# One exponential over both maps' score banks in pass B of the prompt attention

## The chip, the cores and the metric

The kernel runs on one core of a Trainium2 chip. The core has four compute engines that matter here, each with an instruction queue of its own that is worked off in order: TensorE (PE in the profile; its weight loads are PEld), VectorE (DVE), ScalarE (ACT) and GpSimd (POOL). SyncE (SP) issues most DMAs. Engines wait for each other by semaphores. The metric is the device time of one execution in microseconds. Over three runs the kernel before took 2607.59 us (median; 2605.26 to 2613.81).

## The reference, cut to what matters

One step of a hybrid encoder layer: a normalization, one large input projection, two kinds of attention (FoX heads with a cumulative forget bias; differential heads with two softmax maps, a relative bias and a chunk mask), gates, two projections up, one out, a normalization. It is computed for a prompt of 2048 tokens and for 8 sampled sequences of 16 tokens. The change is in the prompt's attention, whose core is, for 8 FoX heads of 64 channels and for 4 differential heads with two maps:

```
s = q . k * SCALE + (c_query - c_key)          # FoX, causal
p = softmax(s); o = p @ v

s_m = q_m . k_m * SCALE + bias(k - q)          # differential, m = 0, 1, masked by chunks of 64
a = softmax(s_0) - lam * softmax(s_1); o = a @ v
```

All arithmetic is in float32; matmul inputs are split into high and low parts where one pass isn't exact enough.

## The kernel before, in words

Three parts follow each other with some overlap: `project` (input projection, the sampled sequences), `prompt_attention`, and `merge` (gates and output). `prompt_attention` works through 8 pairs f. An even f is a pair of FoX heads, an odd f is the two maps of one differential head; in both cases a pair has two maps m = 0, 1. Each pair has 4 blocks of 512 queries (QUERIES), so 32 blocks b.

Pass A takes 128 queries by up to 1024 keys at a time (`A_UNITS`), with queries on partitions, to find each query's maximum (and for differential heads the sum of exponentials): score matmuls in `scores_a` (lines 2064 to 2069) into two PSUM tensors `sa`, band addition (line 1952) and maximum (line 1955) on VectorE, exponential with a sum on ScalarE (line 1891, differential heads only). The result becomes a row added to the queries' data, so that pass B's scores come out already shifted.

Pass B has keys on partitions. A unit u is one block of 512 queries by one tile of 128 keys (`B_UNITS`; 320 of them, 4, 8, 12 and 16 in the four blocks of a pair). For both maps:

1. `scores_b` (lines 2086, 2087): two matmuls a map into `sb_[m]`, a PSUM bank of 512 float32 columns each; near the diagonal only 384 or 256 columns.
2. For differential units near the diagonal (`in_band`, 76 units), VectorE adds a bias band of 256 or 128 columns to each map's scores in place (line 2001).
3. ScalarE writes the exponential of each bank to SBUF, `e[:, u % 6, m]` (line 1924).
4. FoX: GpSimd masks the diagonal square (line 1843), VectorE sums over key tiles (lines 2024, 2027), and `product` multiplies both maps by their values (line 2111). Differential: VectorE combines both maps into `w` (line 2008), and one product follows (line 2108).

There is one pair of banks `sb_`, so unit u + 1 can write bank m only after the exponential of unit u has read it. `e_made` counts exponentials, two a unit, and `scores_b` waits for `2 * u + m - 1`, map by map.

The order on every engine is written out in `events()` (lines 1601 to 1698) as one list that all engines walk through: scores ("B", u) and exponential ("E", u), "W" of unit u - 1, the sums "R" of unit u - 2, as many pass A units ("A", with its exponential "X" one unit later) as a rate asks for, then products. A differential unit's product comes two units later, a FoX unit's in pairs behind every second unit (lines 1686 to 1690).

Of the kernel before, what the change touches and what calls it, by code (L numbers as in the profile page):

```python
# [1481 lines left out]
def prompt_attention(nc, d, keep, link):  # L1482
# [12 lines left out]
    with ExitStack() as space:  # L1495
        s.ctx = space
        with ExitStack() as small:
            s.ctx = small
            with ExitStack() as early:
                lam_prod = Scope(nc, early, "a_", keep).sb("lam_prod", [P, 2, HD])  # L1500
            nmax, total = s.sb("nmax", [P, 2, 2, 8]), s.sb("total", [P, 2, 2, 8])
            nm, gap, log_sum, const = (s.sb(n, [P, 2, 8]) for n in ("nm", "gap", "log_sum", "const"))
            scaled_sum = s.sb("scaled_sum", [P, 2, 8])
            c_hi, c_lo = s.sb("c_hi", [8, P], F32R), s.sb("c_lo", [8, P], F32R)
            ident, ident16 = s.sb("ident", [P, P]), s.sb("ident16", [P, P], BF16)
            lam_in, lam = s.sb("lam_in", [P, 4, HD]), s.sb("lam", [P, 8])
            causal = s.sb("causal", [P, 1, P], BF16)
            v = [s.sb("v0", [P, PROMPT_TILES, P])]
            link["v0"] = v[0]
            run = s.sb("run", [P, 2, MAPS, QUERIES])  # L1510
            ones = s.sb("ones", [P, HD])
            o_raw, o_inv = s.sb("o_raw", [P, QUERIES]), s.sb("o_inv", [P, QUERIES])
        s.ctx = space
        s.sb("space", [P, 6 * D_MODEL])
        maps.append([[s.sb(f"{n}_1{m}", [P, SEQ], F32R) for m in range(MAPS)] for n in ("q1", "k1", "q2", "k2")])
        q1, k1, q2, k2 = ([maps[f][n] for f in range(2)] for n in range(4))
        e = s.sb("e", [P, E_SLOTS, MAPS, QUERIES])
        w = s.sb("w", [P, W_SLOTS, QUERIES])
        o = s.sb("o", [P, 2, QUERIES])
        v.append(s.sb("v1", [P, PROMPT_TILES, P]))  # L1520
        band = s.sb("band", [P, 2, BAND])
        s.sb("space_b", [P, BAND])
        sa = [s.ps(f"sa{i}", [P, CHUNK_KEYS]) for i in range(2)]
        cT = s.ps("cT", [P, 512])
        op = s.ps("op", [P, QUERIES])
        sb_ = [s.ps(f"sb{m}", [P, QUERIES]) for m in range(MAPS)]
    yield

    maps_in = [[s.sem(f"maps_in{f}{m}") for m in range(MAPS)] for f in range(2)]
# [202 lines left out]
    def sync(sp, events):  # L1732
        def load_side(f):

            z = f % 2
            if f % 2:
                for layout in range(2):
                    sp.dma_start(band[:, layout, :], d["band"][layout, f // 2]).then_inc(side_in[z], 16)
            else:
                if f == 0:  # L1740
                    sp.wait_ge(ones_set[0], 4)
                for m in range(MAPS):
                    sp.dma_start(k2[z][m][HD:HD + 2, :].bitcast(F32), d["nck"][f + m]).then_inc(side_in[z], 16)

        def load_map(f, m, n):

            z, hi, lo = f % 2, slice(0, HD), slice(HD, P)
            rows = slice(m * HD, (m + 1) * HD)
            tensor, part, x = ((q1, hi, "q_hi"), (k1, hi, "k_lo"), (q1, lo, "q_lo"), (k1, lo, "k_hi"),
                               (q2, hi, "q_hi"), (k2, hi, "k_hi"))[n]  # L1750
            sp.dma_start(tensor[z][m][part, :].bitcast(F32), d[x][pair_of(f), rows, :]).then_inc(maps_in[z][m], 16)

        def load_v(f):

            z = f % 2
            vsrc, col = d["diff_v_p"] if f % 2 else d["fox_v_p"], f // 2
            if f >= 2:
                sp.wait_ge(multiplied, (f - 1) * NUF)
            sp.dma_start(v[z][:], vsrc.rearrange("(t p) n -> p t n", p=P)
                         [:, :, col * P:(col + 1) * P]).then_inc(v_in[z], 16)  # L1760

        def load(f):

            load_side(f)
            for m in range(MAPS):
                for n in range(6):
                    load_map(f, m, n)
            load_v(f)

        for ev in events:  # L1770
            if ev == ("I", 0):
                sp.dma_start(ident[:], d["ident"]).then_inc(const_in, 16)
                for n, name in enumerate(("lambda_q1", "lambda_k1", "lambda_q2", "lambda_k2")):
                    sp.dma_start(lam_in[:, n, :], d[name].to_broadcast([P, HD])).then_inc(const_in, 16)
            elif ev[0] == "MERGE":
                link["merge"]["sync"](sp, [ev[1]])
            elif ev[0] == "LS":
                load_side(ev[1])
            elif ev[0] == "LM":
                load_map(*ev[1:])  # L1780
            elif ev[0] == "LV":
                load_v(ev[1])
            elif ev == ("I", 1):
                load(1)
            elif ev[0] == "L" and ev[2] == 0:
                f = ev[1]
                sp.wait_ge(b_scored, (f - 1) * 2 * NUF)
                load(f)
            elif ev[0] == "O":
                b = ev[1]  # L1790
                f, Q = b // BLOCKS, b % BLOCKS
                if is_diff(b):
                    sp.wait_ge(o_made, b + 1 - n_total[b + 1])
                else:
                    sp.wait_ge(o_divided, n_total[b + 1])
                sp.dma_start(d["oT"][pair_of(f), :, Q * QUERIES:(Q + 1) * QUERIES], o[:, b % 2, :]).then_inc(stored[b % 2], 16)

    def gpsimd(pool, events):
        for ev in events:
# [33 lines left out]
                pool.wait_ge(o_divided, n_total[b + 1])  # L1833
            elif ev[0] == "E" and on_edge(*B_UNITS[ev[1]]):
                u = ev[1]
                pool.wait_ge(e_made, 2 * u + 2)
                if n_edge[u]:
                    pool.wait_ge(e_masked, n_edge[u])
                else:
# [15 lines left out]
    def scalar(act, events):  # L1855
        for ev in events:
# [52 lines left out]
            elif ev[0] == "E":  # L1909
                u = ev[1]  # L1910
                cols = valid(u)
                for m in range(MAPS):
                    if in_band(*B_UNITS[u]):
                        act.wait_ge(b_biased, 2 * n_band[u] + m + 1)
                    else:
                        act.wait_ge(b_scored, 2 * u + m + 1)
                    if m == 0 and u >= E_SLOTS:

                        if is_diff(B_UNITS[u - E_SLOTS][0]):
                            act.wait_ge(w_made, n_diff[u - E_SLOTS + 1])  # L1920
                        else:
                            act.wait_ge(multiplied, u - E_SLOTS + 1)
                            act.wait_ge(e_added, n_added[u - E_SLOTS + (2 if B_UNITS[u - E_SLOTS][1] == 0 else 1)])
                    nc.scalar.activation(e[:, u % E_SLOTS, m, cols], sb_[m][:, cols], ACT.Exp).then_inc(e_made, 1)  # L1924

    def vector(dve, events):
        for ev in events:
# [65 lines left out]
            elif ev[0] == "E" and in_band(*B_UNITS[ev[1]]):  # L1993
# [2 lines left out]
                lo, hi = max(t0, 0) * P, min(t0 + 2, 4) * P  # L1996
                if t0 <= 0:
                    dve.wait_ge(side_in[1], side_total(B_UNITS[u][0] // BLOCKS))
                for m in range(MAPS):
                    dve.wait_ge(b_scored, 2 * u + m + 1)  # L2000
                    nc.vector.tensor_tensor(sb_[m][:, lo:hi], sb_[m][:, lo:hi], band[:, 1, lo - t0 * P:hi - t0 * P],
                                            ALU.add).then_inc(b_biased, 1)
            elif ev[0] == "W" and is_diff(B_UNITS[ev[1]][0]):
                u = ev[1]
                cols = valid(u)
                dve.wait_ge(e_made, 2 * u + 2)
                dve.wait_ge(multiplied, u - W_SLOTS + 1)
                nc.vector.scalar_tensor_tensor(w[:, u % W_SLOTS, cols], e[:, u % E_SLOTS, 1, cols], lam[:, 5:6],
                                               e[:, u % E_SLOTS, 0, cols], ALU.mult, ALU.add).then_inc(w_made, 1)
            elif ev[0] == "R" and not is_diff(B_UNITS[ev[1]][0]) and B_UNITS[ev[1]][1] > 0:  # L2010
# [1 line left out]
                b, kt = B_UNITS[u]  # L2012
                cols, n = valid(u), n_total[b] % 2
                now, sum_ = e[:, u % E_SLOTS, :, cols], run[:, n, :, cols]
                dve.wait_ge(e_made, 2 * u + 2)
                if on_edge(b, kt):
                    dve.wait_ge(e_masked, n_edge[u + 1])
                if kt == 1:
# [17 lines left out]
    def tensor(pe, events):  # L2036
# [35 lines left out]
        def scores_b(u):  # L2072
# [5 lines left out]
            r = max(0, kt - 4 * Q)  # L2078
            c0 = min(r, 2) * P
            ks = slice(kt * P, (kt + 1) * P)  # L2080
            for m in range(MAPS):
                if u:
                    pe.wait_ge(e_made, 2 * u + m - 1)
                out = sb_[m][:, c0:QUERIES]
                qs = slice(Q * QUERIES + c0, (Q + 1) * QUERIES)
                nc.tensor.matmul(out, k1[z][m][:, ks], q1[z][m][:, qs], start=True, stop=False)  # L2086
                nc.tensor.matmul(out, k2[z][m][0:ROW_C + 2, ks], q2[z][m][0:ROW_C + 2, qs], start=False,  # L2087
                                 stop=True).then_inc(b_scored, 1)

        def product(u):  # L2090
            b, kt = B_UNITS[u]
            z, Q = b // BLOCKS % 2, b % BLOCKS
            if is_diff(b):
                pe.wait_ge(w_made, n_diff[u + 1])
            else:
                pe.wait_ge(e_made, 2 * u + 2)
                if on_edge(b, kt):
                    pe.wait_ge(e_masked, n_edge[u + 1])
            if kt == 0 and b % BLOCKS == 0:
# [48 lines left out]

    def pair_done(sp):

        sp.wait_ge(b_scored, (FT - 1) * 2 * NUF)
        sp.wait_ge(multiplied, (FT - 1) * NUF)

    def first_stored(sp):
# [126 lines left out]
```

## Time and profile before

| | |
|---|---|
| median of 3 runs | 2607.59 us |
| the profiled execution: its own time | 2605.0 us |
| its span, first to last instruction | 2603.2 us |
| mean granted TensorE clock | 0.984 |
| busy: PE, DVE, ACT, POOL | 2478.4, 1374.3, 942.9, 386.0 us |
| line 1924 (pass B's exponentials) | 640 instructions, 310.4 us |
| line 2001 (pass B's band additions) | 152 instructions |
| lines 2086 and 2087 (pass B's scores) | 640 each, 276.5 and 237.1 us |

The profile is of one execution. Times of instructions are from the hardware's records; the ends of matmuls are modelled, since they are pipelined, and the busy time of an engine counts what overlaps once. Pass B runs from 1312 to 2196 us of the span. A clock of 1.00 is 2.4 GHz; the granted clock has two levels, 2.4 and 1.2 GHz, and a number between is the mean over a stretch.

### The profile page before, as it was taken

The page shows a single profiled execution, that of the slowest core. Times are in us where ns is not written, and L with a number is a line of the kernel's source. Part 1 is how long each engine was busy: PE and PEld are TensorE (multiplying, and loading weights), DVE is VectorE, ACT ScalarE, POOL GpSimd, SP SyncE. Part 2 cuts the span into 40 slices and gives each one's busy share as a digit, 9 for nine tenths or more (in the row PEclk, how much of TensorE's full clock was granted, in tenths as well). Part 3 has the DMA queues.
Part 4 walks back from the last instruction along what each step waited for, and adds up shares of the span by engine and source line. Part 5 has one row for each costly group of instructions (what it writes and reads, how often), then busy time and mean ns, then how long its engine had stood idle before and what let it go on. Part 6 is the DMA issues. An engine that isn't in the chain of part 4 may idle for free.

```text
span 2603.2 us, 35097 instructions
## 1 busy us (share of the span) xinstructions
PE 2478.4 (95%) x13569; PEld 1977.2 (76%) x13569; DVE 1374.3 (53%) x2227; ACT 942.9 (36%) x1869; POOL 386.0 (15%) x398
## 2 busy tenths in 40 slices
PE   7999999999999999999988899899899989999998
PEld 5788888789999999999855565565565556888897
DVE  5311123315443333542368888788788786655553
ACT  4123331112222222111136645654664666322221
POOL 0100001121100000112352113103212242000000
PEclk9999999999999999999989999999999999999999
DMA  5688888958987666888560523235054023544432
GB/s 153 161 223 207 202 210 206 209 138 243 244 237 226 207 215 181 233 206 175 145 158 9 126 50 89 55 77 130 5 131 107 28 83 108 181 133 130 143 118 89
DMA packets 583892, 388.65 MB, mean 149 GB/s; under 512 B 318672, under 2 KB 538776, under 8 KB 577416
## 3 DMA queue, kind: packets, MB, share of 16 engines
q1 hardware_dynamic: 574592, 367.80, 53.8%
q0 software_dynamic: 9136, 18.63, 2.1%
q8 instruction: 107, 1.75, 0.3%
q14 instruction: 57, 0.47, 0.1%
HBM read 284.83 MB, written 134.79 MB: 161 GB/s over the span
## 4 chain that ended last, share of the span: by engine, by line
PE 75%; DVE 6%; SPq 5%; ACT 5%; issue 4%; DMA 3%; POOL 1%; DVEq 0%; ACTq 0%; POOLq 0%
PE p_acc L876 13%; PE p_acc L881 12%; PE p_acc L880 12%; PE a_op L2111 5%; PE a_sb L2086 4%; PE a_sb L2087 3%; PE a_op L2108 3%; PE a_sa L2064 2%; PE a_sa L2067 2%; PE e_U L1428 2%; PE e_U L1430 2%; PE e_U L1429 2%; ACT a_e L1924 2%; DVE a_nmax L1955 2%; PE a_sa L2065 2%
## 5 line engine op out<-in xcount | busy, mean ns | idle before, releaser
L876 PE MATMUL p_acc<-p_h_hi,p_w_hi 128*128 128x384 f32 (+1 forms) x1960 | 716.1, 365 | 11.9 <-DVE p_ev L586 5.5
L881 PE MATMUL p_acc<-p_h_hi,p_w_lo 128*128 128x384 f32 (+1 forms) x1920 | 688.0, 358 | 0.0
L880 PE MATMUL p_acc<-p_h_lo,p_w_hi 128*128 128x384 f32 (+1 forms) x1920 | 687.8, 358 | 0.0
L1955 DVE TENSOR_REDUCE a_nmax<-a_sa 128x1 f32<-128x1024 f32 (+7 forms) x384 | 347.2, 911 | 125.0 <-PE a_sa L2069 45.1
L1924 ACT ACTIVATE a_e<-a_sb 128x512 f32<-128x512 f32 (+3 forms) x640 | 310.4, 533 | 278.5 <-PE a_sb L2087 183.8
L876 PEld LDWEIGHTS p_acc<-p_h_hi,p_w_hi 128*128 128x128 f32 x1960 | 370.8, 189 | 52.7 <-issue 12.8
L881 PEld LDWEIGHTS p_acc<-p_h_hi,p_w_lo 128*128 128x128 f32 x1920 | 362.1, 189 | 30.4
L880 PEld LDWEIGHTS p_acc<-p_h_lo,p_w_hi 128*128 128x128 f32 x1920 | 362.6, 189 | 29.0
L692 DVE TENSOR_TENSOR p_w_lo<-p_raw,p_w_hi 128x1024 fp32r<-128x1024 f32 x96 | 125.6, 1308 | 368.8 <-ACT p_w_hi L619 368.7
L2086 PE MATMUL a_sb<-a_q,a_k 128*128 128x512 f32 (+2 forms) x640 | 276.5, 436 | 20.6 <-ACT a_e L1924 18.1
L2087 PE MATMUL a_sb<-a_q,a_k 68*128 68x512 f32 (+2 forms) x640 | 237.1, 374 | 0.0
L619 ACT CAST p_w_hi<-p_raw 128x1024 fp32r<-128x1024 f32 x98 | 102.4, 1045 | 337.8 <-DMA p_raw<-in_w_in 253.4
L599 POOL TENSOR_SCALAR p_ev_hi<-p_ev 128x896 fp32r<-128x896 f32 (+1 forms) x32 | 35.6, 1113 | 1164.3 <-DVE p_ev L586 910.5
L2086 PEld LDWEIGHTS a_sb<-a_q,a_k 128*128 128x128 f32 x640 | 124.0, 194 | 107.6 <-ACT a_e L1924 52.4
L1891 ACT ACTIVATE a_sa<-a_sa,a_nmax 128x1024 f32<-128x1024 f32 (+4 forms) x192 | 162.3, 846 | 51.8 <-DVE a_nmax L1955 50.7
L2064 PE MATMUL a_sa<-a_k,a_q 128*128 128x512 f32 (+4 forms) x320 | 131.5, 413 | 41.3 <-ACT a_sa L1891 41.2
L2111 PE MATMUL a_op<-a_e,a_v 128*64 128x512 f32 (+3 forms) x640 | 145.9, 570 | 3.6 <-issue 3.6
L2108 PE MATMUL a_op<-a_w,a_v 128*128 128x512 f32 (+3 forms) x320 | 147.1, 541 | 1.3 <-ACT a_o_raw L1883 0.8
L2087 PEld LDWEIGHTS a_sb<-a_q,a_k 68*128 68x128 f32 x640 | 124.2, 194 | 23.1 <-issue 10.1
L574 ACT ACTIVATE p_ev<-p_acc 128x384 f32<-128x384 f32 (+1 forms) x80 | 42.8, 534 | 271.9 <-PE p_acc L881 271.8
L2064 PEld LDWEIGHTS a_sa<-a_k,a_q 128*128 128x128 f32 x320 | 61.7, 193 | 100.4 <-ACT a_sa L1891 76.9
L2027 DVE TENSOR_TENSOR a_run<-a_run,a_e 128x1024 f32<-128x1024 f32 (+3 forms) x128 | 137.2, 1072 | 0.6
(233 smaller groups left out, 3475.6 us busy)
## 6 DMA issues: line engine op xcount, KB each, us to landing
p_raw<-in_w_in SPq DMA_DIRECT2D x98, 512.0 KB, 5.7
s_k_raw<-scratch_kS SPq DMA_DIRECT2D x64, 512.0 KB, 6.9
scratch_kS<-in_cache_fox_k SPq DMA_DIRECT2D x32, 512.0 KB, 6.6
scratch_kS<-in_cache_diff_k SPq DMA_DIRECT2D x32, 512.0 KB, 6.4
s_v_raw<-in_cache_fox_v SPq DMA_DIRECT2D x8, 2048.0 KB, 11.0
s_v_raw<-in_cache_diff_v SPq DMA_DIRECT2D x8, 2048.0 KB, 10.0
a_q<-scratch_q_hi SPq DMA_DIRECT2D x32, 512.0 KB, 13.3
a_k<-scratch_k_hi SPq DMA_DIRECT2D x32, 512.0 KB, 15.2
```

Source lines behind the costliest of these rows:

```text
L876: nc.tensor.matmul(acc[a % 2][:, 0:n], hi, h_hi[p][:, k, at:at + n], start=(k == 0), stop=False)
L880: nc.tensor.matmul(acc[a % 2][:, 0:n], hi, h_lo[p][:, k, at:at + n], start=False, stop=False)
L881: last = nc.tensor.matmul(acc[a % 2][:, 0:n], lo, h_hi[p][:, k, at:at + n], start=False, stop=(k == DK - 1))
L1891: nc.scalar.activation(scores_of(ev[1]), scores_of(ev[1]), ACT.Exp, bias=nmax[:, b % 2, c, col:col + 1], accum_out=total[:, b % 2, c, col: ...
L1924: nc.scalar.activation(e[:, u % E_SLOTS, m, cols], sb_[m][:, cols], ACT.Exp).then_inc(e_made, 1)
L1955: nc.vector.tensor_reduce(nmax[:, b % 2, c, col:col + 1], scores_of(ev[1]), axes, ALU.max, negate=True).then_inc(a_maxed, 1)
L2027: nc.vector.tensor_tensor(sum_, sum_, now, ALU.add).then_inc(e_added, 1)
L2064: nc.tensor.matmul(out, q1[z][m][:, qs], k1[z][m][:, k0:k0 + wide], start=True, stop=False)
L2086: nc.tensor.matmul(out, k1[z][m][:, ks], q1[z][m][:, qs], start=True, stop=False)
L2087: nc.tensor.matmul(out, k2[z][m][0:ROW_C + 2, ks], q2[z][m][0:ROW_C + 2, qs], start=False, stop=True).then_inc(b_scored, 1)
L2108: last = nc.tensor.matmul(op[:, cols], v[z][:, kt, :], w[:, u % W_SLOTS, cols], start=(kt == 0), stop=final)
L2111: last = nc.tensor.matmul(op[m * HD:(m + 1) * HD, cols], v[z][:, kt, m * HD:(m + 1) * HD], e[:, u % E_SLOTS, m, cols], start=(kt == 0), st ...
```

## The change

The two score banks become one tensor `sb` of 2 x 512 columns over two adjacent banks. One exponential instruction reads both maps and writes both; one band addition covers both maps, its band operand repeated for the second. The score matmuls are the same four, but one semaphore count, after the last, stands for the unit, and one wait, for the whole exponential of the unit before, stands ahead of the first. Counts of `b_scored`, `e_made` and `b_biased` are halved where they are waited for.

```diff
-        sb_ = [s.ps(f"sb{m}", [P, QUERIES]) for m in range(MAPS)]
+        sb_ = s.ps("sb", [P, MAPS, QUERIES])
...
-                for m in range(MAPS):
-                    if in_band(*B_UNITS[u]):
-                        act.wait_ge(b_biased, 2 * n_band[u] + m + 1)
+                if in_band(*B_UNITS[u]):
+                    act.wait_ge(b_biased, n_band[u + 1])
+                else:
+                    act.wait_ge(b_scored, u + 1)
...
-                    nc.scalar.activation(e[:, u % E_SLOTS, m, cols], sb_[m][:, cols], ACT.Exp).then_inc(e_made, 1)
+                nc.scalar.activation(e[:, u % E_SLOTS, :, cols], sb_[:, :, cols], ACT.Exp).then_inc(e_made, 1)
...
-                for m in range(MAPS):
-                    dve.wait_ge(b_scored, 2 * u + m + 1)
-                    nc.vector.tensor_tensor(sb_[m][:, lo:hi], sb_[m][:, lo:hi], band[:, 1, lo - t0 * P:hi - t0 * P],
-                                            ALU.add).then_inc(b_biased, 1)
+                dve.wait_ge(b_scored, u + 1)
+                bias = band[:, 1:2, lo - t0 * P:hi - t0 * P].to_broadcast([P, MAPS, hi - lo])
+                nc.vector.tensor_tensor(sb_[:, :, lo:hi], sb_[:, :, lo:hi], bias, ALU.add).then_inc(b_biased, 1)
...
+            if u:
+                pe.wait_ge(e_made, u)
             for m in range(MAPS):
-                if u:
-                    pe.wait_ge(e_made, 2 * u + m - 1)
-                out = sb_[m][:, c0:QUERIES]
+                out = sb_[:, m, c0:QUERIES]
...
-                nc.tensor.matmul(out, k2[z][m][0:ROW_C + 2, ks], q2[z][m][0:ROW_C + 2, qs], start=False,
-                                 stop=True).then_inc(b_scored, 1)
+                last = nc.tensor.matmul(out, k2[z][m][0:ROW_C + 2, ks], q2[z][m][0:ROW_C + 2, qs], start=False,
+                                 stop=True)
+            last.then_inc(b_scored, 1)
```

The other edits put `u + 1` for `2 * u + 2` and `NUF` for `2 * NUF` in the waits of GpSimd's mask, VectorE's `w` and sums, the products and SyncE's loads.

## Rows read from the trace of the kernel before

**Rows 1.** The page, part 1: busy time, share of the span, instructions.
```profile
span 2603.2 us, 35097 instructions
PE 2478.4 (95%) x13569; PEld 1977.2 (76%) x13569; DVE 1374.3 (53%) x2227; ACT 942.9 (36%) x1869; POOL 386.0 (15%) x398
```

**Rows 2.** Busy time by stretch, pass B; us busy (instructions) per engine, clock, DMA.
```profile
1312.00:2196.00 884.00, 808.24 (x3374) 488.49 (x3374) 716.37 (x1132) 520.77 (x1134) 227.15 (x275) 0.97 0.34 81
```

**Rows 3.** Waits of TensorE in that stretch: us in total, times, longest.
```profile
PE a_sa L2064 <- ACT a_sa L1891: 41.2, 49, 1.9
PE a_sb L2086 <- ACT a_e L1924: 18.1, 29, 1.2
...
PE a_op L2111 <- issue: 3.6, 1, 3.6
...
PE a_sb L2086 <- DMA a_q<-a_c_lo: 2.3, 1, 2.3
```

**Rows 4.** Groups by line and shape, same stretch: count | busy us, mean ns.
```profile
L1924 ACT ACTIVATE a_e<-a_sb 128x512 f32<-128x512 f32 x448 | 243.7, 597 | 190.0 <-PE a_sb L2087 141.9 <-DVE a_sb L2001 47.4
...
L1891 ACT ACTIVATE a_sa<-a_sa,a_nmax 128x1024 f32<-128x1024 f32 x80 | 87.8, 1097 | 9.1 <-DVE a_nmax L1955 8.8
...
L2001 DVE TENSOR_TENSOR a_sb<-a_sb,a_band 128x256 f32<-128x256 f32 x96 | 37.5, 425 | 5.0 <-PE a_sb L2087 4.5
...
L1924 ACT ACTIVATE a_e<-a_sb 128x384 f32<-128x384 f32 x64 | 28.6, 491 | 25.1 <-PE a_sb L2087 13.8 <-DVE a_sb L2001 10.6
...
L2001 DVE TENSOR_TENSOR a_sb<-a_sb,a_band 128x128 f32<-128x128 f32 x56 | 15.0, 293 | 4.0 <-PE a_sb L2087 2.3
...
L1891 ACT ACTIVATE a_sa<-a_sa,a_nmax 128x512 f32<-128x512 f32 x16 | 10.6, 664 | 6.3 <-DVE a_nmax L1955 6.3
```

**Rows 5.** Timeline, two FoX gaps: start us, us, engine, line.
```profile
1423.25 0.40 PE L2087 MATMUL a_sb<-a_q,a_k 68*128 68x512 f32 x1
...
1424.65 0.40 PE L2087 MATMUL a_sb<-a_q,a_k 68*128 68x512 f32 x1
...
1425.09 1.08 ACT L1924 ACTIVATE a_e<-a_sb 128x512 f32<-128x512 f32 x2 [0.33 <-PE a_sb L2087]
1425.12 0.40 PE L2087 MATMUL a_sb<-a_q,a_k 68*128 68x512 f32 x1
...
1425.80 1.94 PE L2111 MATMUL a_op<-a_e,a_v 128*64 128x512 f32 x8
```

**Rows 6.** Timeline, a differential gap with products alone.
```profile
1490.21 0.39 PE L2087 MATMUL a_sb<-a_q,a_k 68*128 68x512 f32 x1
...
1490.44 1.02 PE L2108 MATMUL a_op<-a_w,a_v 128*128 128x512 f32 x2
...
1491.53 0.39 PE L2087 MATMUL a_sb<-a_q,a_k 68*128 68x512 f32 x1
```

**Rows 7.** Timeline, a gap of a banded differential unit.
```profile
1499.08 0.40 PE L2087 MATMUL a_sb<-a_q,a_k 68*128 68x512 f32 x1
...
1499.12 0.83 DVE L2001 TENSOR_TENSOR a_sb<-a_sb,a_band 128x256 f32<-128x256 f32 x2
...
1501.06 0.34 PE L2087 MATMUL a_sb<-a_q,a_k 68*128 68x384 f32 x1
```

**Rows 8.** Timeline, TensorE released by an exponential (first row: ScalarE's alone).
```profile
1362.11 0.62 ACT L1924 ACTIVATE a_e<-a_sb 128x512 f32<-128x512 f32 x1
...
1362.78 0.50 PE L2086 MATMUL a_sb<-a_q,a_k 128*128 128x512 f32 x1 [0.78 <-ACT a_e L1924]
...
1363.12 0.40 PE L2087 MATMUL a_sb<-a_q,a_k 68*128 68x512 f32 x1
```

**Rows 9.** Busy time by stretch, as rows 2: pass B's start, and behind it.
```profile
1312.00:1441.00 129.00, 112.48 (x484) 64.11 (x484) 100.61 (x131) 69.97 (x156) 51.73 (x52) 0.93 0.32 75
...
2210.00:2590.00 380.00, 376.10 (x1935) 337.57 (x1936) 203.29 (x415) 106.79 (x259) 19.70 (x35) 1.00 0.43 136
```

More of the change, by code:

```diff
@@ L1786, in sync @@
                 f = ev[1]
-                sp.wait_ge(b_scored, (f - 1) * 2 * NUF)
+                sp.wait_ge(b_scored, (f - 1) * NUF)
                 load(f)
@@ L1835, in gpsimd @@
                 u = ev[1]
-                pool.wait_ge(e_made, 2 * u + 2)
+                pool.wait_ge(e_made, u + 1)
                 if n_edge[u]:
@@ L1911, in scalar @@
                 cols = valid(u)
-                for m in range(MAPS):
-                    if in_band(*B_UNITS[u]):
-                        act.wait_ge(b_biased, 2 * n_band[u] + m + 1)
-                    else:
[L1916 to L1923, printed above, removed]
-                    nc.scalar.activation(e[:, u % E_SLOTS, m, cols], sb_[m][:, cols], ACT.Exp).then_inc(e_made, 1)
+                if in_band(*B_UNITS[u]):
+                    act.wait_ge(b_biased, n_band[u + 1])
+                else:
+                    act.wait_ge(b_scored, u + 1)
+                if u >= E_SLOTS:
+                    if is_diff(B_UNITS[u - E_SLOTS][0]):
+                        act.wait_ge(w_made, n_diff[u - E_SLOTS + 1])
+                    else:
+                        act.wait_ge(multiplied, u - E_SLOTS + 1)
+                        act.wait_ge(e_added, n_added[u - E_SLOTS + (2 if B_UNITS[u - E_SLOTS][1] == 0 else 1)])
+                nc.scalar.activation(e[:, u % E_SLOTS, :, cols], sb_[:, :, cols], ACT.Exp).then_inc(e_made, 1)
     def vector(dve, events):
@@ L2005, in vector @@
                 cols = valid(u)
-                dve.wait_ge(e_made, 2 * u + 2)
+                dve.wait_ge(e_made, u + 1)
                 dve.wait_ge(multiplied, u - W_SLOTS + 1)
@@ L2014, in vector @@
                 now, sum_ = e[:, u % E_SLOTS, :, cols], run[:, n, :, cols]
-                dve.wait_ge(e_made, 2 * u + 2)
+                dve.wait_ge(e_made, u + 1)
                 if on_edge(b, kt):
@@ L2095, in product @@
             else:
-                pe.wait_ge(e_made, 2 * u + 2)
+                pe.wait_ge(e_made, u + 1)
                 if on_edge(b, kt):
@@ L2149, in pair_done @@
     def pair_done(sp):
-        sp.wait_ge(b_scored, (FT - 1) * 2 * NUF)
+        sp.wait_ge(b_scored, (FT - 1) * NUF)
         sp.wait_ge(multiplied, (FT - 1) * NUF)
```

## The prediction

> **What bounds the kernel now.** I read the page first. TensorE is busy for 95% of the span, ScalarE for 36% [rows 1], so what a change does to the time is what it does to TensorE's queue. The changed instructions (lines 1924, 2001, 2086, 2087) all lie between 1312 and 2196 us, the stretch in which pass B runs its 320 units. The busy times of that stretch alone come next: TensorE 808.2 of 884 us, VectorE 716.4, ScalarE 520.8 [rows 2]. TensorE therefore stands idle there for 884.0 - 808.2 = 75.8 us, and has 2.76 us a unit; VectorE follows closely, ScalarE has room. Third, the waits of TensorE in the stretch: 41.2 us for pass A's exponentials (line 1891), only 18.1 us for pass B's own exponentials (line 1924) [rows 3]. Today the two score banks work as a pair. While ScalarE exponentiates bank 0, TensorE fills bank 1, and it may fill bank 0 for the next unit while bank 1 is exponentiated. So a unit's exponentials are nearly over when TensorE is through with its scores: the pair of them starts at 1425.09, 0.03 us before the last score matmul starts, and ends 0.65 us after that matmul's end [rows 5].
>
> **The change, part by part.**
>
> *The exponential.* 640 instructions become 320. One of 512 columns takes 597 ns, one of 384 takes 491 [rows 4]: 106 ns for 128 columns. A fused one of 2 x 512 is then 597 + 4 x 106 = 1021 ns; from pass A's two sizes (1097 less 664 = 433 ns for 512 columns, [rows 4]) it is 1030. I take 1.03 us. The ends are 1.02 and the 1.10 of pass A's own instruction. The pair takes 1.08 today [rows 5], so ScalarE is relieved by 0.05 us a unit, 16 us in all, of an engine that is busy for 59% of the stretch: worth nothing on the path by itself.
>
> *The waits.* This is where the cost is. The exponential of a unit can't start before all four score matmuls, and the next unit's scores can't start before it is over. Behind the waiting score matmul, in TensorE's queue, stand the other map's scores, pass A's next scores and the value products; behind pass A's scores VectorE's maxima wait. What TensorE can still do meanwhile is what the written order puts between two score blocks: pass A's scores and products. To price one gap I measure from the end of a unit's last score matmul to the end of the next unit's first line-2087 matmul (ends, because the recorded start of a matmul in a full stream lies early). The change needs for it: 0.04 us until ScalarE starts (first-map scores end 1425.05, the pair starts 1425.09, [rows 5]); 1.03 for the exponential; 0.05 until TensorE restarts (an exponential ends at 1362.11 + 0.62 = 1362.73, the released matmul starts at 1362.78); 0.74 for the two matmuls (1362.78 to 1363.12 + 0.40) [rows 8]. That is 1.86 us for a full-width unit. What each kind of gap has today:
>
> FoX unit without a product behind it [rows 5]: 1423.25 + 0.40 = 1423.65 to 1424.65 + 0.40 = 1425.05, so 1.40 us, 0.46 too little. The next gap of the same rows holds the eight product matmuls of two units (1.94 us) and covers everything; so it is with every second FoX unit. Differential unit with products alone [rows 6]: 1490.60 to 1491.92, 1.32 us, 0.54 too little. With pass A's scores as well the gap is mostly between 1.6 and 2.1, where the price is small or nothing.
>
> *The band addition.* In a banded unit it stands between scores and exponential. 425 ns for 256 columns, 293 for 128 [rows 4], so 132 ns for 128 more, and 0.69 us for 2 x 256. Two take 0.83 today [rows 7]. VectorE saves 0.14 us in most of the 76 banded units, some 10 us of its 716. But the first addition now starts after the second map's scores. In rows 7 the gap runs from 1499.48 to 1501.40, 1.92 us; needed are 0.04 + 0.69 + 0.06 between the engines (estimated from the lag of ScalarE behind TensorE, above) + 1.03 + 0.05 + 0.63 (narrower matmuls) = 2.50: 0.58 too little. Where VectorE is late anyway with its maxima, less is lost.
>
> *The sum.* I went through the timeline gap by gap for all 319, with the needs above cut to each unit's width, and with ScalarE's and VectorE's earlier work where it ends later than the scores:
> FoX, 160 gaps: 62 are too short, on average 1.26 us where 1.75 is needed: 30.8 us.
> Differential without band, 84 gaps: 45 too short, 1.62 against 1.95: 14.8 us.
> Differential with band, 75 gaps: 51 too short, 1.94 against 2.41: 23.9 us.
> Together 69.5 us in 158 gaps; the other 161 cost nothing. It takes the place of nothing: the present waits on line 1924 are inside the measured gaps.
>
> *What hangs on it.* (a) A unit's last exponential ends 0.04 + 1.03 = 1.07 us behind the scores and not 0.65, so pass A's exponential, next in ScalarE's queue, starts 0.42 us later. TensorE waits for that one 49 times, for 41.2 us [rows 3]. Bounds: nothing where VectorE's maximum is the later one, 49 x 0.42 = 21 us if never; I take 6. (b) Idle time of TensorE that a delay eats up, because its releaser does not move: GpSimd's mask before the first product (3.6 us), DMA (2.3), [rows 3]. Bounds 0 and, if pass A's waits gave way too, 47 us; I take 5, since those waits stand behind the very exponentials that move. (c) The clock. The granted clock is 0.93 of full speed in the stretch with 13% of TensorE's time idle, 1.00 where it is 1% [rows 9]: part of such a stretch runs at 1.2 instead of 2.4 GHz. Bounds: nothing, and 23 us if the time at the lower level doubles with the idle time (0.03 of 884 us lost today). I take 5.
> DMA, SP's and GpSimd's instructions stay; their waits are renumbered and come at the same point of the work, or 0.4 us later for the mask, which is used two units on.
>
> Sum: 69.5 + 6 - 5 + 5 = 75.5 us. The profiled execution took 2605.0 us (span 2603.2): 2680.5. The median of the runs lies 2.6 above it, so the forecast is 2683 us.
>
> The row for ScalarE shows 59% of the stretch. On this the Trainium skill, "Perfetto Trace Analysis", section "Optimizing Scalar/DVE Operations", says two things: grouping into larger operations helps throughput if the engine is saturated, and if it isn't but makes bubbles on other engines, breaking instructions up may let work finish sooner. By the first alone the sum would be the 16 us of relief; by the second it is the loss above. The trace bears out the second: the released engine is the full one.
>
> **The rivals.**
> *A: the cover holds (not slower).* ScalarE and VectorE set the pace: TensorE's 75.8 us of idle time and VectorE's 81% speak for it. Then the shorter queues are what counts: 49 waits x 0.05 = 2 us, and 10 us of band additions: 2593 to 2608. It decides where a gap is longer than its need; against it stand 158 gaps that aren't.
> *B: half eaten up.* Later units find their other waits gone: the 57.7 us of TensorE's idle time that isn't for line 1924 falls by half, 29 us in place of (b)'s 5: 2683 - 24 = 2659. Against it: delay ahead of pass A's scores delays their exponentials too.
> *C: the delay multiplies.* ScalarE's queue carries it: (a) at 21 us, and each FoX gap with pass A's work becomes ScalarE-bound: about 15 + 15 more, 2713.
> *D: the clock.* With idle time twice today's, TensorE stays at 1.2 GHz twice as long: (c) at 23, 2701. For it, the 0.93 of rows 9.
> The Trainium skill, "TensorE: Matmul & The Clock Gate", section "A second HAM failure mode: psum-queue depth-cycling", tells of the same case: short idle spells between groups of matmuls that cycle through PSUM make the clock swing between its two levels. Rows 9 show both levels, but not yet that spells under a microsecond bring the lower one.
>
> **How the numbers follow.** Forecast 0.60, A 0.04, B 0.14, C 0.10, D 0.12. The likeliest gives 2683. Low end: B's absorption and nothing for (a) and (c): 2607.6 + 69.5 - 29 - 5 = 2643. High end: C with two thirds of D's 18 us: 2725. Some 2 in 10 are left outside, A among them. A measurement of this kernel tells some 0.3% (8 us) from no change. Only A reaches that near: slower 0.95, same 0.03, faster 0.02.
>
> **What would show it.** The wait of line 2086 on line 1924 grows from 18 us to 80 or more, in single waits of 0.3 to 0.9 us, in FoX units every second one; the fused exponential lasts 1.02 to 1.04 us at full width; TensorE's idle time in the stretch rises to 145 to 155 us with the same matmul work; the stretches before 1312 us and after pass B keep their length. The forecast is wrong if the wait of line 2086 stays under 40 us, if pass A's wait (41.2 us) falls by more than it says, or if the clock in the stretch falls under 0.94.

## The result, and the profile after

The changed kernel takes 2694.64 us (median of 4 runs, 2687.03 to 2702.71) against 2609.54 for the kernel before in the same comparison: ratio 1.0327, 95% interval 1.0306 to 1.0348, so 85 us slower. The forecast was 2683.

The page, part 1, answers to [rows 1]:

```profile
span 2688.7 us, 34701 instructions
PE 2515.7 (94%) x13569; PEld 1985.1 (74%) x13569; DVE 1374.5 (51%) x2151; ACT 920.2 (34%) x1549; POOL 380.8 (14%) x398
```

The matmuls are as many as before, ScalarE has 320 instructions fewer, VectorE 76, and the span is 85.5 us longer. Pass B now runs from 1312 to 2282 us. Busy time by stretch (columns as in [rows 2]) and TensorE's waits in it (as [rows 3]):

```profile
1312.00:2282.00 970.00, 846.03 (x3375) 497.96 (x3374) 714.83 (x1057) 497.52 (x813) 221.77 (x275) 0.94 0.31 74
```

```profile
PE a_sb L2084 <- ACT a_e L1923: 66.6, 118, 1.4
PE a_sa L2062 <- ACT a_sa L1891: 42.6, 33, 2.6
...
PE a_sa L2065 <- DVE a_nmax L1954: 3.7, 4, 1.1
```

The stretch is 86 us longer than in [rows 2], all of the loss. TensorE's wait for pass B's exponentials grows from 18.1 us in 29 waits to 66.6 in 118. But TensorE's idle time grows only by 48 us (75.8 to 124.0). The other 38 us are recorded as busy time: the same matmuls take longer. Part of that is the clock, 0.94 where it was 0.97; summed over its steps TensorE spends 109 us of the stretch at 1.2 GHz and spent 61. Half of that increase lies in the first pair of heads (41 us against 17), where the clock was 0.93 in [rows 9]:

```profile
1312.00:1458.00 146.00, 124.18 (x481) 69.66 (x480) 100.99 (x131) 66.08 (x115) 49.63 (x52) 0.86 0.28 66
```

The groups by line and shape, as [rows 4]:

```profile
L1923 ACT ACTIVATE a_e<-a_sb 128x1024 f32<-128x1024 f32 x224 | 229.5, 1024 | 287.6 <-PE a_sb L2085 222.3 <-DVE a_sb L2000 60.9 <-DVE a_w L2006 3.9
...
L2000 DVE TENSOR_TENSOR a_sb<-a_sb,a_band 128x512 f32<-128x512 f32 x48 | 33.4, 696 | 22.3 <-PE a_sb L2085 21.8
```

The full-width exponential takes 1024 ns and the full-width addition 696, where 1030 and 689 had been worked out.

The first gap of [rows 5] in the timeline after (block 3, key tile 10, counted from 0; rows left out are marked):

```profile
1439.07 0.40 PE L2085 MATMUL a_sb<-a_q,a_k 68*128 68x512 f32 x1
...
1439.50 1.02 ACT L1923 ACTIVATE a_e<-a_sb 128x1024 f32<-128x1024 f32 x1 [1.11 <-PE a_sb L2085]
...
1439.77 0.40 PE L2062 MATMUL a_sa<-a_k,a_q 128*128 128x512 f32 x1
...
1440.00 0.39 PE L2063 MATMUL a_sa<-a_k,a_q 66*128 66x512 f32 x1
1440.42 0.44 ACT L1891 ACTIVATE a_sa<-a_sa,a_nmax 128x256 f32<-128x256 f32 x1
...
1440.58 0.50 PE L2084 MATMUL a_sb<-a_q,a_k 128*128 128x512 f32 x1 [0.19 <-ACT a_e L1923]
...
1440.91 0.40 PE L2085 MATMUL a_sb<-a_q,a_k 68*128 68x512 f32 x1
```

From the last score's end (1439.07 + 0.40) to the end of the next unit's first map (1440.91 + 0.40) it is 1.84 us, where it was 1.40 and 1.86 was said to be needed. TensorE has its pass A scores in that time and then nothing, and 0.19 us is all that the row names as waiting. The rest is hidden in how matmuls are recorded. In a full stream they start 0.23 us apart though each is recorded as 0.40 long (1439.77 and 1440.00), so the record before a pause covers some 0.17 us of it; and the released matmul is recorded as 0.50 us and not 0.40. So a loss of 0.44 us shows as 0.19 us of wait. The same in the gap of [rows 6]:

```profile
1509.76 0.40 PE L2085 MATMUL a_sb<-a_q,a_k 68*128 68x512 f32 x1
...
1510.20 1.02 ACT L1923 ACTIVATE a_e<-a_sb 128x1024 f32<-128x1024 f32 x1 [1.20 <-PE a_sb L2085]
...
1511.27 0.50 PE L2084 MATMUL a_sb<-a_q,a_k 128*128 128x512 f32 x1 [0.25 <-ACT a_e L1923]
1511.62 0.40 PE L2085 MATMUL a_sb<-a_q,a_k 68*128 68x512 f32 x1
```

1510.16 to 1512.02 is 1.86 us (1.32 before). And the banded gap of [rows 7]:

```profile
1519.68 0.40 PE L2085 MATMUL a_sb<-a_q,a_k 68*128 68x512 f32 x1
...
1520.19 0.70 DVE L2000 TENSOR_TENSOR a_sb<-a_sb,a_band 128x512 f32<-128x512 f32 x1 [0.85 <-PE a_sb L2085]
...
1520.92 1.02 ACT L1923 ACTIVATE a_e<-a_sb 128x1024 f32<-128x1024 f32 x1 [2.11 <-DVE a_sb L2000]
...
1522.28 0.34 PE L2085 MATMUL a_sb<-a_q,a_k 68*128 68x384 f32 x1
```

1520.08 to 1522.62 is 2.54 us (1.92 before; 2.50 said).

### The profile page after: what moved, and what is told of

Read it like the earlier page. It is cut to its first block, busy times and chain, and to the rows that moved or that the text cites. A ratio compares the mean times of both kernels' runs of the same rounds, so it can differ in the third digit from the quotient of the medians.

```text
span 2688.7 us, 34701 instructions
## 1 busy us (share of the span) xinstructions
PE 2515.7 (94%) x13569; PEld 1985.1 (74%) x13569; DVE 1374.5 (51%) x2151; ACT 920.2 (34%) x1549; POOL 380.8 (14%) x398
## 4 chain that ended last, share of the span: by engine, by line
PE 71%; ACT 7%; SPq 7%; DVE 6%; issue 4%; DMA 3%; POOL 1%; DVEq 0%; ACTq 0%; POOLq 0%
PE p_acc L876 11%; PE p_acc L881 11%; PE p_acc L880 11%; PE a_sb L2084 5%; PE a_op L2110 5%; ACT a_e L1923 5%; PE a_sb L2085 4%; SPq L355 3%; PE a_sa L2062 2%; PE e_U L1428 2%; PE e_U L1430 2%; PE e_U L1429 2%; PE a_op L2107 2%; PE a_sa L2065 2%; DVE a_nmax L1954 2%
## 5 line engine op out<-in xcount | busy, mean ns | idle before, releaser
L1923 ACT ACTIVATE a_e<-a_sb 128x1024 f32<-128x1024 f32 (+1 forms) x320 | 286.7, 896 | 402.6 <-PE a_sb L2085 278.5
L881 PEld LDWEIGHTS p_acc<-p_h_hi,p_w_lo 128*128 128x128 f32 x1920 | 362.0, 189 | 30.7
L2084 PE MATMUL a_sb<-a_q,a_k 128*128 128x512 f32 (+2 forms) x640 | 270.0, 426 | 67.6 <-ACT a_e L1923 66.6
L2062 PE MATMUL a_sa<-a_k,a_q 128*128 128x512 f32 (+4 forms) x320 | 133.3, 418 | 44.1 <-ACT a_sa L1891 42.6
L2110 PE MATMUL a_op<-a_e,a_v 128*64 128x512 f32 (+3 forms) x640 | 156.2, 605 | 2.7 <-issue 2.7
L2085 PEld LDWEIGHTS a_sb<-a_q,a_k 68*128 68x128 f32 x640 | 126.0, 197 | 16.1 <-issue 2.7
```

Of the source, the lines that this page charges most:

```text
L881: last = nc.tensor.matmul(acc[a % 2][:, 0:n], lo, h_hi[p][:, k, at:at + n], start=False, stop=(k == DK - 1))
L1923: nc.scalar.activation(e[:, u % E_SLOTS, :, cols], sb_[:, :, cols], ACT.Exp).then_inc(e_made, 1)
L2062: nc.tensor.matmul(out, q1[z][m][:, qs], k1[z][m][:, k0:k0 + wide], start=True, stop=False)
L2085: last = nc.tensor.matmul(out, k2[z][m][0:ROW_C + 2, ks], q2[z][m][0:ROW_C + 2, qs], start=False, stop=True)
L2110: last = nc.tensor.matmul(op[m * HD:(m + 1) * HD, cols], v[z][:, kt, m * HD:(m + 1) * HD], e[:, u % E_SLOTS, m, cols], start=(kt == 0), st ...
```

## The experiments

Two theories were tried throughout. G: a gap costs what the chain "scores, exponential, scores" needs beyond the work that TensorE has there. Q: the later exponential pushes back pass A's exponentials in ScalarE's queue, and these hold TensorE. The expectations name further ones where they are tried; the letters C and D there aren't the prediction's rivals. Times are medians; ratios are to the kernel before. Times at 1.2 GHz and idle times are TensorE's in pass B of the profiled execution, summed from its trace.

**e1_release**, half of the waiting:
```diff
-                    pe.wait_ge(e_made, 2 * u + m - 1)
+                    pe.wait_ge(e_made, 2 * u)
```


> The kernel before with one edit: the next unit's scores wait for both of this unit's exponentials; the exponentials stay two, each after its own map's scores. Theory G (gaps: what counts is whether TensorE's written work between two score blocks is longer than the chain that must run there): the last exponential ends 0.65 us after the scores, so 0.65 + 0.05 + 0.74 = 1.44 us are needed in place of the 1.86 of the full change; going through the gaps of the trace before gives 35 us in 109 gaps, and with the slower clock that idle time brings, 40 to 52 us over before. Rival Q (the cost comes from the later exponential, which pushes pass A's exponential back in ScalarE's queue): the exponentials don't move here, so under 15 us.

2634.99 us, ratio 1.0107 (1.0089 to 1.0125): 28 us over before. That is more than Q's 15 and well under G's 40 to 52. In the trace the gaps that need more than before did grow as G said: those called short for the full change, where the clock stayed at 2.4 GHz, by 34.9 us. What G left out is that the others, again at 2.4 GHz, shrank by 10.6 us, and the wait for pass A's exponentials with them (41.2 to 34.4 us). Nor does the clock go with the waiting: 15.0 of the trace's extra time fall in the first pair, where TensorE was idle for 1.8 us more than before (18.3 against 16.5) but ran at 1.2 GHz for 44.4 us instead of 17.1.

**e2_start**, the other half:
```diff
-                        act.wait_ge(b_biased, 2 * n_band[u] + m + 1)
+                        act.wait_ge(b_biased, 2 * n_band[u] + 2)
...
-                        act.wait_ge(b_scored, 2 * u + m + 1)
+                        act.wait_ge(b_scored, 2 * u + 2)
...
-                    dve.wait_ge(b_scored, 2 * u + m + 1)
+                    dve.wait_ge(b_scored, 2 * u + 2)
```


> The kernel before with the other half: both exponentials (and both band additions) wait for both maps' scores, but remain two instructions, and the next unit's scores wait map by map. Theory G: the first exponential ends 0.04 + 0.60 us after the scores and the second at 1.12; needed in the gap are 1.43 to 1.44 us, as in the other half: 35 us without and 40 to 52 with the clock. Rival Q: this half moves pass A's exponentials as the full change does, so most of the full change's 85 us, 60 or more.

2655.17 us, ratio 1.0186 (1.0165 to 1.0206): 48 us over before, inside G's range and short of Q's 60. But G alone gives both halves the same price, and this one costs 20 us more. TensorE's waits in pass B, first of this kernel and then of e1_release, say where:

```profile
PE a_sa L2064 <- ACT a_sa L1891: 53.8, 57, 2.7
PE a_sb L2086 <- ACT a_e L1924: 29.8, 57, 1.2
```

```profile
PE a_sb L2086 <- ACT a_e L1924: 38.4, 62, 1.5
PE a_sa L2064 <- ACT a_sa L1891: 34.4, 33, 1.9
```

Starting later lifts the wait for pass A's exponential (line 1891) from 41.2 to 53.8 us; releasing later doesn't, it even falls. So the push that Q speaks of exists, and it is the smaller part.

**e3_both**, both edits above together.


> Both halves of the waiting, but two exponentials and two band additions as before: the full change without its merging of instructions. Theory G: needed are 0.04 + 1.08 + 0.05 + 0.74 = 1.91 us, 0.05 more than with one instruction, and 0.14 more in banded units: 8 to 15 us slower than the changed kernel, about 2705 us. Rival M (the merged instruction itself is what costs, by its longer hold of both banks): faster than the changed kernel, 2650 us or less.

2711.15 us, ratio 1.0400 (1.0375 to 1.0425), 104 us over before. The halves alone add up to 76. By G's needs that is expected: the FoX gap of 1.40 us is only 0.04 short for either half (1.44) and 0.51 short for both (1.91). The merged instructions themselves give back 16 to 19 us: 2711.15 less 2694.64, or, by the ratios, 1.0400 here and 1.0327 (1.0306 to 1.0348) with them, times 2607. G had said 8 to 15, a little too low; M, by which the merged instruction is what costs, is out.

**e4_cover**, one exponential only where the gap was long enough:
```diff
+    FUSED = frozenset([0, 2, 3, 5, 7, 9, ...])    # 162 units
+    n_exp = list(itertools.accumulate([0] + [1 if u in FUSED else 2 for u in range(NU)]))
...
+                for m in ([slice(0, MAPS)] if u in FUSED else range(MAPS)):
...
+                    pe.wait_ge(e_made, n_exp[u] - (0 if u - 1 in FUSED else 1 - m))
```


> One exponential for both maps only in the 162 units behind which the trace before shows a gap long enough; two, with the waits of before, in the other 158; band additions two everywhere. Theory G: within 8 us of before (2600 to 2618). Rival Q: the later exponentials of half the units still push pass A's back: 20 to 40 us over before.

2624.46 us, ratio 1.0065 (1.0048 to 1.0083): 17 us over before, above G's range and below Q's. TensorE's wait for pass B's exponentials is what it was; that for pass A's rises:

```profile
PE a_sa L2067 <- ACT a_sa L1893: 47.8, 51, 2.2
PE a_sb L2089 <- ACT a_e L1927: 18.1, 29, 1.2
```

The gaps were rightly told apart: in the trace the 158 short ones together grew by 0.4 us and the 161 others by 18.0. So a covered gap isn't free: the wait for pass A's exponentials takes 7 us more. Most of the loss goes with the clock: the time at 1.2 GHz goes from 61 to 89 us, and gaps in which either trace shows that level hold 12.9 us of the growth.

**e5_fill**, matmuls that nothing reads, in the changed kernel's idle time (FILL: 1 to 3 for a unit, by the shortfall):
```diff
+            if free[0] is not None and free[1] >= 2 and u in FILL and B_UNITS[u][0] < 28:
...
+                for _ in range(FILL[u]):
+                    nc.tensor.matmul(cT[:, 0:P], ident[:], ident[:], start=True, stop=True)
```


> The changed kernel with idle time of TensorE filled by matmuls that nothing reads: in 76 of the gaps found too short (of the first seven pairs), 1 to 3 extra 128 x 128 float32 matmuls of the identity into a free bank, 167 in all, go ahead of the wait for the exponential, about 0.22 us each, sized by the gap's shortfall. Theory C (a good part of the 85 us, about 24, is the lower clock that the idle time brings: 61 us at the lower level in pass B before, 109 after): the time at the lower level falls to 60 to 85 us and the kernel gets 8 to 20 us faster than the changed one, though it does more work. Rival W (the clock follows something else, or the cost of the idle time is the idle time alone): no change or up to 10 us slower by the added work.

2691.72 us (2687.81 to 2696.90), ratio 1.0337 (1.0314 to 1.0359), the same as without: the 8 to 20 us that theory C promised did not come. The stretch from 1312 us (columns as above), to the end of its pass B:

```profile
1312.00:2281.00 969.00, 870.18 (x3707) 538.47 (x3706) 713.22 (x1056) 497.07 (x813) 222.78 (x275) 0.95 0.31 74
```

24 us more of recorded TensorE work fit in without a microsecond lost, which shows that in these gaps TensorE waits and doesn't work. The named wait for the exponential fell from 66.6 us to 40.2, the time at 1.2 GHz only from 109 to 102:

```profile
PE a_sb L2095 <- ACT a_e L1923: 40.2, 66, 1.4
```

So the run doesn't show what lifts the clock, and whether the idle time in the short gaps brings the lower level stays open.

**e6_after_even**, **e7_before_even**: another order of the FoX products, in the changed kernel and in the kernel before.
```diff
-            elif u >= 3 and u % 2:
-                multiply(u - 3)
+            elif u >= 2:
                 multiply(u - 2)
```


> The changed kernel with another order: a FoX unit's product follows two units after its scores, one product in every gap, instead of two products in every second gap. The arithmetic is the same. Theory G: every FoX gap grows to 1.26 + 0.93 = 2.2 us where 1.75 is needed on average, so the FoX price (30.8 us of the 69.5 us walked through, and its part of the clock, about 10) goes: 2645 to 2665 us. Rival Q (the ScalarE queue decides): the order of products doesn't touch it, 2685 to 2695.

2640.75 us, ratio 1.0137 (1.0117 to 1.0156): 54 us less than the changed kernel, at the same arithmetic, same exponentials and same waits. It is 4 us below G's 2645 to 2665: G had put some 10 us for the clock, but the time at 1.2 GHz fell from 109 to 72 us, which is about 19 us if half of it is lost.

> The same other order of products on the kernel before. Theory G: its need in a gap is small, only the 18 us of waits for the exponentials can shrink, and shorter waits lift the clock a little: 2590 to 2610 us. Rival: two FoX products in a row are worth something by themselves (fewer switches between 64- and 128-column weights); then 10 us slower or more.

2596.80 us, ratio 0.9959 (0.9947 to 0.9971): 10 us faster than the kernel before.

Per pair of heads (from the first score matmul of a pair's pass B to that of the next, worked out from each timeline; even pairs FoX, odd ones differential; of pair 7, to the first score matmul of its last unit), us:

| pair | 0 | 1 | 2 | 3 | 4 | 5 | 6 | 7 |
|---|---|---|---|---|---|---|---|---|
| before | 127.9 | 103.8 | 113.8 | 104.3 | 113.8 | 104.3 | 115.4 | 98.4 |
| changed | 145.7 | 111.3 | 123.8 | 112.2 | 123.7 | 111.3 | 130.0 | 109.9 |
| e6_after_even | 134.2 | 112.2 | 112.8 | 112.3 | 112.7 | 112.3 | 112.8 | 109.9 |
| e7_before_even | 132.0 | 104.4 | 110.2 | 104.6 | 110.3 | 104.7 | 110.2 | 98.5 |

The order of FoX products takes 11 us and more out of each FoX pair of the changed kernel and nothing out of the differential ones. This is the plainest evidence for G. Some of it is the clock: in pairs 2, 4 and 6 TensorE spends 6.8, 6.8 and 19.9 us at 1.2 GHz in the changed kernel and none in e6_after_even, while its idle time falls from 16.1 us to 5.4 or 5.5 in each. TensorE's waits, in e6_after_even and then in e7_before_even:

```profile
PE a_sb L2083 <- ACT a_e L1922: 33.1, 70, 1.4
PE a_sa L2061 <- ACT a_sa L1890: 25.9, 33, 2.0
```

```profile
PE a_sa L2063 <- ACT a_sa L1890: 19.2, 34, 1.5
PE a_cT L2135 <- DVE a_gap L1968: 10.9, 4, 2.7
PE a_sb L2085 <- ACT a_e L1923: 9.2, 13, 1.2
```

The kernel before had the same weakness in small: its wait for line 1924 halves (18.1 to 9.2), and the one for line 1891 does too (41.2 to 19.2). Only the first pair got slower, from 127.9 to 132.0 us, with less idle time (12.1 us for 16.5) and more at 1.2 GHz (30.7 us for 17.1).

**e8_even_late**: e7_before_even, with products two by two kept for the first pair.
```diff
+            elif u >= 2 * BLOCKS * 5:
+                multiply(u - 2)
             elif u >= 3 and u % 2:
```


> The kernel before with one FoX product in every gap, but only from the second pair on; the first pair keeps its products two by two, since its stretch had grown from 127.9 to 132.0 us in the run with the even order throughout, while the later FoX stretches had shrunk by 3.6 to 5 us each. Theory G: the first stretch goes back to 128 us, the others stay: 2592 to 2596 us. Rival: a shift of the start only moves the same loss to a later stretch: 2597 us as with the even order throughout.

2595.93 us, ratio 0.9961 (0.9945 to 0.9976). The first pair goes back to 128.0 us, but differential pairs 1, 3 and 5 take 104.9 to 105.0, and the whole can't be told from e7_before_even. These two are the fastest versions.

**e9_fox_merged**: even order, one exponential in FoX units, two in differential ones (the edit of e4_cover with another set).


> Even order of products throughout, one exponential for both maps in the FoX units only (160), two with the waits of before in the differential units. Theory G: the differential stretches are as before (104.4 us), the FoX ones as in the changed kernel with even order (112.8 against 110.2): 2597 + 3 x 2.6 + 2 = 2605 to 2612 us. Rival Q (later exponentials push pass A's back in ScalarE's queue wherever it has them, which is beside FoX units): 2620 us or more.

2606.85 us, ratio 0.9999 (0.9989 to 1.0008), 10 us over e7_before_even, at the low end of G. With cover in every FoX gap, merging still brings nothing. Not all of the 10 us is shown to be its price: the traces show 2.6 us in each of FoX pairs 2, 4 and 6 (112.8 against 110.2), as G said, but pair 0 is shorter (129.2 against 132.0), and pass B starts 8.1 us later (1316.8 against 1308.7), ahead of everything that the edit touches.

**e10_band**, the band addition merged and nothing else; **e11_exp**, the change without that merging. Of e10_band's edit (the merged addition itself is the change's):
```diff
-                for m in range(MAPS):
-                    dve.wait_ge(b_scored, 2 * u + m + 1)
+                dve.wait_ge(b_scored, 2 * u + 2)
```


> The kernel before with the band additions alone merged (76 instead of 152, over both banks); exponentials two, scores wait map by map. Theory G: in 75 banded gaps the first exponential starts later by up to 0.44 us and the second not at all; the first map's release comes at 0.04 + 0.69 + 0.06 + 0.60 us behind the scores: 5 to 15 us slower. Rival D (VectorE is close to full, so 0.14 us less in each banded unit is what counts): 0 to 10 us faster.

2619.07 us, ratio 1.0048 (1.0032 to 1.0064): 13 us slower, as G said (5 to 15). VectorE's shorter work doesn't pay for the later start.

> The changed kernel with the band additions made two again, each after its own map's scores (one exponential, after both): the exponential part of the change alone. Theory G: the second addition ends 0.43 us after the scores instead of 0.69 for the merged one, if VectorE is free, so up to 0.26 us less is needed in 51 short banded gaps: 2 to 12 us faster than the changed kernel. Rival D: the merged addition is a gain by itself, and the kernel gets up to 10 us slower than the changed one.

2683.14 us, ratio 1.0279 (1.0248 to 1.0310); the change's 1.0327 (1.0306 to 1.0348) overlaps that, so the 11 us between the medians, in G's range of 2 to 12, are likely and not shown.

## Why the prediction was right

The forecast of +75.5 us met +85, by its own mechanism: what each gap lacks is most of the loss. Two sizes were off in opposite directions, so the total came out closer than its terms did. Point by point:

*The exponential and the addition.* 1030 and 689 ns foreseen, 1024 and 696 measured. That merging is worth nothing on the path doesn't hold once the waits are there: on top of them it gives 16 to 19 us back (e3_both against the change), because there the exponential stands in the chain.

*The needs.* 1.86 us for a full-width gap, measured 1.84 and 1.86; 2.50 for the banded one, measured 2.54.

*The sum of gaps.* Both timelines, gap by gap: the FoX gaps called short grew by 38.1 us (30.8 foreseen), the differential ones by 14.9 (14.8), the banded ones by 19.1 (23.9), together 72.1 against 69.5. FoX is furthest off. The banded class came out lower, likely because VectorE, with more time between maxima, is late less often; that isn't shown. The gaps called covered grew by 15.5 us, where nothing was foreseen for them by themselves. This growth is the clock's: of all 319 gaps, 286 show 2.4 GHz alone in both traces, and there the short ones grew by 68.4 us and the covered ones shrank by 5.9. The 33 gaps in which either trace shows 1.2 GHz grew by 25.1 us, 21.2 of them in covered ones.

*(a), the push in ScalarE's queue.* It exists (e2_start, e4_cover): 7 to 13 us in line 1891's waits. In the changed kernel itself that wait is 42.6 us, 1.4 more than before, in fewer and longer waits, so the 6 us put for it isn't found there.

*(b), idle time eaten up.* The 3.6 us wait before the first product, which the prediction put down to GpSimd and for which the row names no releaser, went to 2.7, and the DMA's 2.3 is gone from the list: 3 us of the 5. In all, TensorE's idle time that isn't for pass B's exponential stayed as it was, 57.7 us before and 57.4 after.

*(c), the clock.* This is the mis-sized term. 5 us was put for it; TensorE spent 48 us more at 1.2 GHz (109 against 61), and half of that, some 24 us, is the estimated loss. Two comparisons inside the changed kernel bear this price out. Its executions run from 2687.03 us at a mean clock of 0.977 to 2702.71 at 0.971: 0.006 of 2695 us is 16 us, and they lie 15.7 apart. And in its profile pairs 4 and 6 have 16.1 us of idle time each, but 6.8 and 19.9 us at 1.2 GHz, and take 123.7 and 130.0 us (before, 113.8 and 115.4 us with 3.4 and 6.8 at 1.2 GHz). The prediction's upper bound of 23 us went by the rounded 0.97; with the 61 us at 1.2 GHz summed from the trace, doubling them costs 31. Rival D had named just this. The time at the lower level grew 1.8-fold, the mean clock came to 0.94, the edge that the prediction had set, and the measured 2694.64 lies nearer to D's 2701 than to 2683.

Without its clock term the forecast was 69.5 + 6 - 5 = 70.5 us of waiting, where the gaps at full clock grew by 62.5. So the waiting was put some 4 to 8 us too high and the clock about 20 too low, and that the total is off by only 10 us is in part luck.

Why the clock falls isn't shown. The Trainium skill, "TensorE: Matmul & The Clock Gate", section "A second HAM failure mode: psum-queue depth-cycling", warns of this effect of short idle spells. The traces agree only in part. Idle time and low clock rise together over five kernels (idle 76, 90, 98, 124, 136 us; at 1.2 GHz 61, 85, 96, 109, 119), before, e1_release, e2_start, changed, e3_both. But e7_before_even has 57 us of idle time and 61 at 1.2 GHz like the kernel before, e4_cover 81 and 89, e10_band 84 and 65, e6_after_even 84 and 72; and in the first pairs of e1_release and e7_before_even, and in pairs 4 and 6 above, the time at 1.2 GHz changes without the idle time or against it. e5_fill shows that putting work into some of the gaps isn't enough to undo it.

*The wait named by the profile.* "80 us or more, in single waits of 0.3 to 0.9" was wrong: 66.6 us in 118 waits, 0.56 on average. The step behind it took the whole shortfall for a wait; about 0.25 us of each is recorded as busy. TensorE's idle time is 124 us for the same reason, not 145 to 155.

*The range.* Its low end, 2643, takes (b)'s 5 us off twice, since B's 29 stand in their place; it should be 2648. Nothing hangs on it.

*Rivals.* A (cover holds) is out. B (half eaten up) is out: 57.4 of the 57.7 us are still there. C's push in ScalarE's queue is shown, in a smaller size. D is borne out for its size.

## What to carry to other kernels

Two banks with a semaphore count each are a double buffer even inside one unit of work; merging their reader turns them into a single buffer, and the price per unit is the reader's whole duration plus the latencies and the first refill, less whatever work the written order puts between two fills. Measure that gap on the engine that fills, for each kind of unit, before merging. If some gaps are empty and others double, evening out the order pays with or without the merging: it gave 54 us in the merged kernel and 10 in the other.

## What the runs showed of the hardware

A wait of TensorE of some tenths of a microsecond costs about 0.25 us more than its row names: 0.17 us of the pause lie under the record of the matmul before (0.40 us long, where the next starts 0.23 behind in a full stream), and the released one is recorded 0.1 us longer (0.50 against 0.40). The profile counts both as busy. An estimate from this: pass B has 151 waits on the two exponentials where it had 78, so some 18 to 20 of the 38 us by which its busy time grew are hidden waits; the rest is about what the clock costs.

Time at 1.2 GHz costs about half of itself, and executions of one kernel differ in it: 15.7 us between 2687.03 and 2702.71 us go with a mean clock of 0.977 and 0.971.

And 24 us of extra matmuls in idle gaps cost nothing measurable (e5_fill, 2691.72 against 2694.64 us), but raised the mean clock of the stretch only from 0.94 to 0.95.
